# Taking the first level of the RWKV triangular inverse from the transposed pair matrix

## The chip, the cores and the metric

The kernel runs on one core of a Trainium2 chip. The number reported is the device time of one execution in microseconds (us), as a median of several. The names of the engines in the profile: PE is TensorE (PEld its weight loads), DVE is VectorE, ACT is ScalarE, POOL is GpSimd, SP is the engine that issues most DMAs.

## The reference, cut to what matters

The program is three transformer layers on one sequence of 512 tokens. Two layers are of one kind (mLSTM, gated linear attention, sparse attention); the third has an RWKV-7 branch beside a differential attention branch, then a feed-forward part. The change lies in the RWKV branch, whose core is a recurrence over tokens, run forwards and backwards for 8 heads of width 64:

```
def step(state, inp):
    r_t, w_t, k_t, v_t, kk_t, a_t = inp
    sa = jnp.einsum('bhij,bhj->bhi', state, -kk_t)
    state = (state * w_t[:, :, None, :]
             + sa[..., None] * (kk_t * a_t)[:, :, None, :]
             + v_t[..., None] * k_t[:, :, None, :])
    y_t = jnp.einsum('bhij,bhj->bhi', state, r_t)
    return state, y_t
...
y = (rwkv7_scan(r_h, decay[:, :, 0], k_dir[:, :, 0], v_h, kk, a[:, :, 0], False)
     + rwkv7_scan(r_h, decay[:, :, 1], k_dir[:, :, 1], v_h, kk, a[:, :, 1], True))
```

The kernel does not step through tokens. It cuts the sequence into 8 chunks of 64 tokens. Inside a chunk the feedback of one token on the next is a strictly triangular 64x64 matrix A of inner products (the decayed removal keys, here `kap`, against the decayed replacement keys, here `bet`), and the chunk needs the inverse of I + A.

## The kernel before, in words

**Stages.** The kernel is a chain of stages with a barrier between them. Most stages are large matrix products at full width. `rwkv_stage` is one stage of about 175 us, in which all matrices are small.

**Tiling of the stage.** It has four rounds (`PER = 4`, the loop variable `i`). One round treats two heads for all 8 chunks, in both directions; a direction is a "way", `w.d` 0 or 1, with four PSUM banks each. A tile named `AT`, `BT`, `M`, `MT`, `MbT`, `MkT` or `T1` is 128 partitions by 512 columns: 16 matrices of 64x64, eight side by side in the upper 64 partitions and eight in the lower.

**The head of a round, on PE.** `within` multiplies keys with keys, chunk by chunk. Called at line 1858 with `cols == 2` it makes 64x128 products: first `bet` against `kap` and `rho` together, which gives the transposed pair matrix `AT` (and `MbT`), later `kha` against the same, which gives `BT` and `MkT`. Called at line 1860 it makes the untransposed matrix A, 64x64, into banks 0 and 1. The order on PE is: AT for both ways, A for both ways, BT for both ways (the second after ACT has copied AT out of the banks they share).

**The head on the other engines.** ACT copies AT and BT out of PSUM (line 2111, one instruction of 1024 columns each, semaphores `at_copied`, `bt_copied`). DVE makes the start of the inverse from A: line 2282 multiplies it with the mask of level 0 (the pairs of neighbouring tokens), line 2284 subtracts the result from the identity; `m_ready` then lets PE go on. POOL masks BT in place (line 2193) and, at the start of each round but the first, finishes the state matrices of the round before (lines 2167 and 2168).

**The levels.** The inverse is doubled in five levels. In each, and for both ways: `by_level` (line 1869) multiplies AT and M, DVE masks the product into T1 (line 2289), PE transposes M (line 1885) and ACT copies it to MT (line 2136), `by_inverse` (line 1878) multiplies MT and T1, DVE subtracts from M (line 2295). The last level is done in transposed form (lines 1893 and 2299). Between these stand small products for the round before or after (`beside`).

**The tail.** After the levels come the products with the inverse (line 2038), then a long row of 64x64 products, lines 2051 to 2074, and right behind them the AT products of the next round. ACT copies the results of lines 2071 and 2074 at line 2151 (`gh_copied`), POOL then works on them (lines 2167, 2168).

The order on each engine is the order of the code; the engines meet only at semaphores. `then_inc` counts a semaphore up when the instruction is done, `wait_ge` holds the engine's queue.

Of the kernel before, what the change touches and what calls it, by code (L numbers as in the profile page):

```python
# [8 lines left out]
ALU = mybir.AluOpType  # L9
# [3 lines left out]
P = 128  # L13
# [5 lines left out]
CHUNK = 64  # L19
# [49 lines left out]
class Chain:  # L69


    def __init__(self, eng, sem):
        self.eng, self.sem, self.n = eng, sem, 0
# [20 lines left out]
def by_tile(x):  # L94
    return x.rearrange("p (t n) -> p t n", n=P)
# [1619 lines left out]
HALF = (slice(0, 64), slice(64, 128))  # L1715
# [7 lines left out]
def every(mask):  # L1723

    return mask.rearrange("p (a n) -> p a n", a=1).broadcast_to([P, NCH, CHUNK])
# [16 lines left out]
class Way:  # L1742
# [7 lines left out]
    def __init__(self, m, d):  # L1750
        self.d, self.bank = d, 4 * d
        mats = m.rw_mats[:, 8 * d:8 * d + 8, :]
        self.AT, self.BT, self.M, self.MT, self.MbT, self.MkT, _, self.T1 = (mats[:, n, :] for n in range(8))
        self.AT_MbT, self.BT_MkT = (mats[:, n:n + 5:4, :] for n in range(2))
        self.nPZ = mats[:, 0:2, :].rearrange("p a (t n) -> p (a t) n", n=P)
        self.keys = m.rw_keys[d]
        self.kap, self.bet, self.kha = (self.keys[:, n, :] for n in range(3))
        self.rho = [self.keys[:, 3 + n, :] for n in range(2)]
        self.kap_rho = [self.keys[:, 0:4 + n:3 + n, :] for n in range(2)]
        tok = m.rw_tok[d]  # L1760
        self.cat = tok[:, 0:2, :].rearrange("p a (t n) -> p (a t) n", n=P)
        self.bet_t, self.kha_t = by_tile(tok[:, 2, :]), by_tile(tok[:, 3, :])
        first = m.rw_first[d]
        self.kap_of, self.bet_of, self.kha_of = ((lambda i, n=n: first[n] if i == 0 else self.keys[:, n, :]) for n in range(3))
        self.rho_of = lambda i: first[3] if i == 0 else self.rho[i % 2]
        self.kap_rho_of = lambda i: m.rw_first_pair[d] if i == 0 else self.kap_rho[i % 2]
        self.sg, self.a, self.cum = m.rw_temps[d]
        self.ex_in, self.ex_neg = m.tmp[:, 2 * d, :], m.tmp[:, 2 * d + 1, :]
        self.ex = self.sg if d == 0 else m.rs[:, 2, :]
        self.g, self.h = m.rw_gh[d]  # L1770
        self.gh = m.arena[:, 34 + d:38 + d:2, :]
        self.strict, self.incl = (m.cstrict_f, m.cincl_f) if d == 0 else (m.cstrict_b, m.cincl_b)
        self.levT = (m.clevel_b, m.clevel_f)[d]

    def at(self, n):

# [21 lines left out]
def pair_place(c):  # L1798

    return 64 * (2 * (c % T) + c // T)  # L1800


def turn_of(t):

    return 2 * (t % 2) + t // 2
# [12 lines left out]
def rwkv_stage(nc, m, ahead):  # L1818
# [4 lines left out]
    ways = [Way(m, 0), Way(m, 1)]  # L1823
    ch = chunked
    PER = 4
    SCAN_AT, EX_AT = (4, 6), (12, 16)

    names = ("at_ready", "at_copied", "a_ready", "bt_ready", "bt_copied", "bt_masked", "mb_masked", "mk_masked", "bv_ready", "bv_copied",
             "m_ready", "mt_ready", "t1_ready", "t1_copied", "x_ready", "xt_ready", "pz_ready", "pz_copied",
             "ry_ready", "ry_taken", "gh_ready", "gh_copied", "gh_taken", "k_ready", "kha_ready", "rate_ready", "ex_ready", "exp_ready",  # L1830
             "tok_ready")
    with stage(nc, "dve_own", "pool_own", "lora_ready", "turn_ready", "sig_ready", "gs_ready", "s_ready", "yi_ready", "yi_taken",
# [12 lines left out]
        def _(pe):  # L1845
            def bank(w, n):
                return m.ps[:, w.bank + n, :]

            def within(w, banks, lhsT, rhs, cols):

                for t in range(T):
                    for p, hh in QUADS:
                        c = 2 * t + p
                        cs, at = slice(c * 64, c * 64 + 64), turn_of(t) * P
                        ps = slice(pair_place(c), pair_place(c) + 64)
                        if cols == 2:
                            out = m.ps[HALF[p], w.bank + banks[hh], at:at + P].rearrange("p (a n) -> p a n", a=2)
                            ins = pe.matmul(out, lhsT[HALF[hh], cs], rhs[HALF[hh], :, ps], start=True, stop=True)
                        else:
                            ins = pe.matmul(m.ps[HALF[p], w.bank + banks[hh], at:at + 64], lhsT[HALF[hh], ps], rhs[HALF[hh], cs],  # L1860
                                            start=True, stop=True)
                return ins

            def by_level(w):

                for j in range(T):
                    for p, h in QUADS:
                        cols = slice(64 * (2 * j + h), 64 * (2 * j + h) + 64)
                        ins = pe.matmul(m.ps[HALF[h], w.bank + p, 64 * j:64 * j + 64], w.AT[HALF[p], cols], w.M[HALF[p], cols],
                                        start=True, stop=True)  # L1870
                return ins
# [123 lines left out]
            for i in range(PER):  # L1995
                more = i + 1 < PER
                for w in ways:
                    if i:
                        pe.wait_ge(sem[f"k_ready{w.d}"], 3 * i)
                        pe.wait_ge(sem[f"ry_taken{w.d}"], 2 * i)  # L2000
                    within(w, (2, 3), w.bet_of(i), w.kap_rho_of(i), 2).then_inc(sem[f"at_ready{w.d}"], 1)
                for w in ways:
                    if i:
                        pe.wait_ge(sem[f"gh_copied{w.d}"], i)
                    within(w, (0, 1), w.kap_of(i), w.bet_of(i), 1).then_inc(sem[f"a_ready{w.d}"], 1)
                for w in ways:
                    pe.wait_ge(sem[f"at_copied{w.d}"], i + 1)
                    if i:
                        pe.wait_ge(sem[f"kha_ready{w.d}"], i)
                    within(w, (2, 3), w.kha_of(i), w.kap_rho_of(i), 2).then_inc(sem[f"bt_ready{w.d}"], 1)  # L2010
                for n in range(1, LAST + 1):
                    for w in ways:
                        pe.wait_ge(sem[f"m_ready{w.d}"], LAST * i + n)
                        by_level(w).then_inc(sem[f"t1_ready{w.d}"], 1)
                        if n == 1:
                            pe.wait_ge(sem[f"bt_copied{w.d}"], i + 1)
                        if w.d == 1 and n in (2, 3) and more:
                            pe.wait_ge(sem["sig_ready"], 4 * i + 2 * (n - 1))
                        if n == 4 + w.d:
                            pe.wait_ge(sem[f"bv_copied{w.d}"], i + 1)  # L2020
                        turned_inverse(w).then_inc(sem[f"xt_ready{w.d}"], 1)
                    beside(i, 2 * n - 2)
                    for w in ways:
                        pe.wait_ge(sem[f"t1_copied{w.d}"], LAST * i + n)
                        pe.wait_ge(sem[f"mt_ready{w.d}"], (LAST + 1) * i + n)
                        if n < LAST:
                            by_inverse(w).then_inc(sem[f"x_ready{w.d}"], 1)
                        else:
                            transposed(w).then_inc(sem[f"xt_ready{w.d}"], 1)
                    beside(i, 2 * n - 1)  # L2030
                for w in ways:
# [3 lines left out]
                    for j in range(T):  # L2035
                        for h, p in QUADS:
                            x = 2 * j + p
                            ins = pe.matmul(m.ps[HALF[p], w.bank + h, j * P:j * P + P],
                                            w.MT[HALF[h], 64 * x:64 * x + 64], w.cat[HALF[h], x, :], start=True, stop=True)
                    ins.then_inc(sem[f"pz_ready{w.d}"], 1)  # L2040
                for w in ways:
# [11 lines left out]
                    for t in range(T):  # L2053
# [4 lines left out]
                        for p, hh in QUADS:  # L2058
                            ins = pe.matmul(m.ps[HALF[hh], w.bank + 2 + p, 256 + t * 64:320 + t * 64],
                                            w.nPZ[HALF[p], at_slot(hh, t), 64:P],  # L2060
                                            w.MbT[HALF[p], 256 * hh + 64 * turn_of(t):256 * hh + 64 * turn_of(t) + 64], start=False, stop=True)
                    ins.then_inc(sem[f"ry_ready{w.d}"], 1)
                for w in ways:
# [5 lines left out]
                    for t in range(T):  # L2069
# [3 lines left out]
                        for p, hh in QUADS:  # L2073
                            ins = pe.matmul(m.ps[HALF[hh], w.bank + p, 256 + t * 64:320 + t * 64], w.bet_t[HALF[p], t, HALF[hh]],
                                            w.nPZ[HALF[p], at_slot(hh, t), 64:P], start=False, stop=True)
# [134 lines left out]
        def _(dve):  # L2210
            own = Chain(dve, sem["dve_own"])
            eye = every(m.eye64)
# [64 lines left out]
            dve.tensor_scalar(m.cols[:, 24:28], m.c2("k_a", 4), -1.0, 1.0, ALU.mult, ALU.add).then_inc(sem["rest_ready"], 1)  # L2277
            for i in range(PER):
                for w in ways:
                    a = m.ps[:, w.bank:w.bank + 2, :].rearrange("p a (t x n) -> p (a t) x n", x=2, n=64)  # L2280
                    dve.wait_ge(sem[f"a_ready{w.d}"], i + 1)
                    own.op(dve.tensor_tensor(ch(w.M), a[:, :, 0, :], every(w.levT[:, 0:64]), ALU.mult))
                    own.wait()
                    dve.tensor_tensor(ch(w.M), eye, ch(w.M), ALU.subtract).then_inc(sem[f"m_ready{w.d}"], 1)
                for n in range(1, LAST + 1):
                    for w in ways:
                        mask = w.levT[:, n * 64:n * 64 + 64].rearrange("q (a j n) -> q a j n", a=1, j=1).broadcast_to([P, 2, T, CHUNK])
# [871 lines left out]
```

## Time and profile before

| what | value |
|---|---|
| median of 3 runs | 2307.98 us (2306.52 to 2308.14) |
| the profiled execution's own time | 2306.07 us |
| its span, first to last instruction | 2304.3 us |
| outside the span | 1.8 us |
| PE busy | 2214.3 us, 96% |
| DVE, ACT, POOL busy | 1139.4, 967.9, 926.4 us |
| the stage of the change | from about 1358 to 1533 us of the span |

Times in the rows are microseconds from the start of the span, unless they are marked ns. In a timeline row the first number is the start, the second the time from the first start to the last end of the group, and `xN` the number of instructions in it. Each matmul of 32-bit numbers that the code writes stands twice in the trace: 16 matmuls of 64x64 are `x32`. A wait in brackets is idle time before the row, with what ended it; "issue" is idle time that the profile can lay on no other engine.

### The profile page before, as it was taken

The page shows a single profiled execution, that of the slowest core. Times are in us where ns is not written, and L with a number is a line of the kernel's source. Part 1 is how long each engine was busy: PE and PEld are TensorE (multiplying, and loading weights), DVE is VectorE, ACT ScalarE, POOL GpSimd, SP SyncE. Part 2 cuts the span into 40 slices and gives each one's busy share as a digit, 9 for nine tenths or more (in the row PEclk, how much of TensorE's full clock was granted, in tenths as well). Part 3 has the DMA queues.
Part 4 walks back from the last instruction along what each step waited for, and adds up shares of the span by engine and source line. Part 5 has one row for each costly group of instructions (what it writes and reads, how often), then busy time and mean ns, then how long its engine had stood idle before and what let it go on. Part 6 is the DMA issues. An engine that isn't in the chain of part 4 may idle for free. (4 is left out here: it accounts for less than half of the span.)

```text
span 2304.3 us, 36016 instructions
## 1 busy us (share of the span) xinstructions
PE 2214.3 (96%) x14926; PEld 1713.3 (74%) x14926; DVE 1139.4 (49%) x1925; ACT 967.9 (42%) x1384; POOL 926.4 (40%) x705
## 2 busy tenths in 40 slices
PE   7999999999999999999999988879999999999997
PEld 5776777787877857767878777767666788888885
DVE  5554843344246549342443686644544757216425
ACT  5433355445354233553452445534367242222243
POOL 4342243334543413433345445533332455445453
PEclk9999999999999999999999999999999999999998
DMA  4221222222322302222132300012121233323322
GB/s 155 86 92 37 68 88 74 64 74 80 97 83 79 95 19 85 89 65 73 65 106 92 101 20 4 4 31 84 64 65 55 92 97 97 100 92 101 100 92 73
DMA packets 50558, 175.03 MB, mean 76 GB/s; under 512 B 6036, under 2 KB 7004, under 8 KB 50396
## 3 DMA queue, kind: packets, MB, share of 16 engines
q1 hardware_dynamic: 50396, 172.73, 23.5%
q8 instruction: 118, 1.93, 0.3%
q14 instruction: 44, 0.36, 0.0%
HBM read 170.60 MB, written 2.11 MB: 75 GB/s over the span
## 5 line engine op out<-in xcount | busy, mean ns | idle before, releaser
L349 POOL TENSOR_TENSOR w_low<-work,w_high 128x512 fp32r<-128x512 f32 x622 | 834.9, 1363 | 1243.1 <-ACT w_high L298 1243.1
L279 PE MATMUL ps<-x_high_tiles,w_high 128*128 128x512 f32 x1544 | 624.5, 404 | 18.0 <-POOL w_low L349 11.5
L298 ACT ACTIVATE w_high<-work 128x1024 fp32r<-128x1024 f32 x311 | 329.3, 1059 | 734.2 <-PE ps L279 730.4
L279 PE MATMUL ps<-x_low_tiles,w_high 128*128 128x512 f32 x1544 | 603.7, 391 | 0.8 <-DVE x_low_tiles L371 0.8
L279 PE MATMUL ps<-x_high_tiles,w_low 128*128 128x512 f32 x1544 | 603.4, 391 | 0.0
L279 PE MATMUL ps<-arena_parts,w_high 128*128 128x512 f32 x1264 | 397.6, 391 | 4.3 <-DVE arena L437 1.6
L279 PEld LDWEIGHTS ps<-x_high_tiles,w_high 128*128 128x128 f32 x1544 | 290.8, 188 | 119.2 <-issue 44.6
L279 PEld LDWEIGHTS ps<-x_low_tiles,w_high 128*128 128x128 f32 x1544 | 290.7, 188 | 64.2 <-DVE x_low_tiles L371 1.6
L279 PEld LDWEIGHTS ps<-x_high_tiles,w_low 128*128 128x128 f32 x1544 | 291.2, 189 | 63.1 <-issue 6.0
L279 PEld LDWEIGHTS ps<-arena_parts,w_high 128*128 128x128 f32 x1264 | 237.3, 188 | 56.8 <-issue 3.2
L279 PE MATMUL ps<-arena_parts,w_low 128*128 128x512 f32 x608 | 236.6, 389 | 0.0
L441 DVE TENSOR_TENSOR xT_sb<-ps,xT_sb 128x512 f32<-128x512 f32 x40 | 27.6, 691 | 249.3 <-PE ps L279 249.3
L279 PEld LDWEIGHTS ps<-arena_parts,w_low 128*128 128x128 f32 x608 | 114.2, 188 | 24.1 <-issue 0.7
L279 PE MATMUL ps<-w_high,x_high_tiles 128*128 128x512 f32 x288 | 118.2, 410 | 2.6 <-POOL w_low L349 2.6
L279 PE MATMUL ps<-w_high,x_low_tiles 128*128 128x512 f32 x288 | 112.4, 390 | 0.0
L279 PE MATMUL ps<-w_low,x_high_tiles 128*128 128x512 f32 x288 | 112.3, 390 | 0.0
L437 DVE TENSOR_TENSOR arena<-ps,arena 128x512 f32<-128x512 f32 x32 | 22.1, 691 | 123.2 <-ACT ps L436 123.2
L835 DVE SCALAR_TENSOR_TENSOR arena<-ps,small,arena 128x511 f32<-128x511 f32 (+2 forms) x96 | 71.9, 749 | 3.4
L279 PEld LDWEIGHTS ps<-w_high,x_high_tiles 128*128 128x128 f32 x288 | 54.0, 188 | 25.6 <-issue 11.0
L422 ACT ACTIVATE arena<-ps 128x512 f32<-128x512 f32 x84 | 47.9, 596 | 59.1 <-PE ps L279 59.0
L831 DVE TENSOR_SCALAR arena<-ps,small 128x512 f32<-128x512 f32 x32 | 25.8, 807 | 76.2 <-PE ps L279 76.2
L279 PEld LDWEIGHTS ps<-w_low,x_high_tiles 128*128 128x128 f32 x288 | 54.1, 188 | 12.5 <-issue 2.2
(446 smaller groups left out, 2790.5 us busy)
## 6 DMA issues: line engine op xcount, KB each, us to landing
work<-w_first SPq DMA_DIRECT2D x178, 512.0 KB, 3.6
work<-w_second SPq DMA_DIRECT2D x134, 512.0 KB, 3.6
xT_sb<-xT SPq DMA_DIRECT2D x8, 256.0 KB, 6.6
outT<-arena SPq DMA_DIRECT2D x8, 256.0 KB, 2.1
arena<-distance_bias SPq DMA_DIRECT2D x4, 256.0 KB
small<-small SPq DMA_DIRECT2D x1, 815.5 KB, 5.1
arena<-consts SPq DMA_DIRECT2D x1, 544.0 KB, 3.7
base<-consts SPq DMA_DIRECT2D x1, 512.0 KB
```

The source lines that it names most:

```text
L279: ins = pe.matmul(out, lhsT, rhs, start=(n == 0 and k == 0 and q == 0), stop=(n == unit["granules"] - 1 and k == len(ops[i]) - 1 and q == 2))
L298: act.activation(m.wh[:, split_of(g), :], m.raw[:, raw_of(g), :], ACT.Copy).then_inc(sem["high_ready"], 1)
L349: pool.tensor_tensor(m.wl[:, split_of(g), part], m.raw[:, raw_of(g), part], m.wh[:, split_of(g), part].bitcast(F32), ALU.subtract).then_in ...
L422: return dict(act=lambda e, ps: e.activation(dst, ps, ACT.Copy))
L437: dve=lambda e, ps, own: e.tensor_tensor(dst, ps, dst, ALU.mult))
L441: return dict(dve=lambda e, ps, own: e.tensor_tensor(dst, ps, dst, ALU.add))
L831: own.op(dve.tensor_scalar(acc, ps, cw[:, 48 + i:49 + i], cb[:, i:i + 1], ALU.mult, ALU.add))
L835: ins = dve.scalar_tensor_tensor(out=acc[:, back:S], in0=ps[:, 0:S - back], scalar=c, in1=acc[:, back:S], op0=ALU.mult, op1=ALU.add)
```

## The change

The untransposed products and their semaphore `a_ready` go. DVE takes the transposed matrix `AT` that ACT has copied, masks it with the level-0 mask of the other orientation (`lev0`), subtracts it from the identity into T1, and transposes T1 into M by its 32x32 block transpose. All that is not zero there lies in 2x2 blocks on the diagonal, so that transposing every 32x32 block in place is the transpose of each 64x64 matrix. The work on the two ways is interleaved: both masks, both subtractions, both transposes. PE's wait for `gh_copied` (ACT has emptied banks 0 and 1 of the round before) moves from the products of A to the first level.

```diff
-        self.levT = (m.clevel_b, m.clevel_f)[d]
+        self.levT, self.lev0 = (m.clevel_b, m.clevel_f)[d], (m.clevel_f, m.clevel_b)[d][:, 0:CHUNK]
...
                 for w in ways:
                     if i:
                         pe.wait_ge(sem[f"k_ready{w.d}"], 3 * i)
                         pe.wait_ge(sem[f"ry_taken{w.d}"], 2 * i)
-                    within(w, (2, 3), w.bet_of(i), w.kap_rho_of(i), 2).then_inc(sem[f"at_ready{w.d}"], 1)
-                for w in ways:
-                    if i:
-                        pe.wait_ge(sem[f"gh_copied{w.d}"], i)
-                    within(w, (0, 1), w.kap_of(i), w.bet_of(i), 1).then_inc(sem[f"a_ready{w.d}"], 1)
+                    within(w, w.bet_of(i), w.kap_rho_of(i)).then_inc(sem[f"at_ready{w.d}"], 1)
                 for w in ways:
                     pe.wait_ge(sem[f"at_copied{w.d}"], i + 1)
...
-                    within(w, (2, 3), w.kha_of(i), w.kap_rho_of(i), 2).then_inc(sem[f"bt_ready{w.d}"], 1)
+                    within(w, w.kha_of(i), w.kap_rho_of(i)).then_inc(sem[f"bt_ready{w.d}"], 1)
                 for n in range(1, LAST + 1):
                     for w in ways:
                         pe.wait_ge(sem[f"m_ready{w.d}"], LAST * i + n)
+                        if n == 1 and i:
+                            pe.wait_ge(sem[f"gh_copied{w.d}"], i)
                         by_level(w).then_inc(sem[f"t1_ready{w.d}"], 1)
...
             for i in range(PER):
                 for w in ways:
-                    a = m.ps[:, w.bank:w.bank + 2, :].rearrange("p a (t x n) -> p (a t) x n", x=2, n=64)
-                    dve.wait_ge(sem[f"a_ready{w.d}"], i + 1)
-                    own.op(dve.tensor_tensor(ch(w.M), a[:, :, 0, :], every(w.levT[:, 0:64]), ALU.mult))
-                    own.wait()
-                    dve.tensor_tensor(ch(w.M), eye, ch(w.M), ALU.subtract).then_inc(sem[f"m_ready{w.d}"], 1)
+                    dve.wait_ge(sem[f"at_copied{w.d}"], i + 1)
+                    dve.tensor_tensor(ch(w.T1), ch(w.AT), every(w.lev0), ALU.mult).then_inc(sem[f"pairs_ready{w.d}"], 1)
+                for w in ways:
+                    dve.wait_ge(sem[f"pairs_ready{w.d}"], 2 * i + 1)
+                    dve.tensor_tensor(ch(w.T1), eye, ch(w.T1), ALU.subtract).then_inc(sem[f"pairs_ready{w.d}"], 1)
+                for w in ways:
+                    dve.wait_ge(sem[f"pairs_ready{w.d}"], 2 * i + 2)
+                    dve.transpose(w.M, w.T1).then_inc(sem[f"m_ready{w.d}"], 1)
```

On PE, at the head of the second round, this stood (`ps` is PSUM, `work` holds the keys and matrices; here a matmul of the code counts once):

```order
L2074 MATMUL ps<-work,arena 64x64 x4
L1858 MATMUL ps<-work 64x128 x32
L1860 MATMUL ps<-work 64x64 x32
L1858 MATMUL ps<-work 64x128 x32
L1869 MATMUL ps<-work 64x64 x16
L1885 MATMUL ps<-base,work 128x128 x4
```

and this stands now, with line 1857 for 1858, 1865 for 1869, 1881 for 1885 and 2068 for 2074:

```order
L2068 MATMUL ps<-work,arena 64x64 x4
L1857 MATMUL ps<-work 64x128 x64
L1865 MATMUL ps<-work 64x64 x16
L1881 MATMUL ps<-base,work 128x128 x4
```

The 32 products of A are gone, and the BT products stand right behind the AT products. On DVE, at the same place, stood:

```order
L2282 TENSOR_TENSOR work<-ps,arena 128x512
L2284 TENSOR_TENSOR work<-arena,work 128x512
L2282 TENSOR_TENSOR work<-ps,arena 128x512
L2284 TENSOR_TENSOR work<-arena,work 128x512
L2289 TENSOR_TENSOR work<-ps,arena 128x2x4x64 x2
```

and now stands:

```order
L2275 TENSOR_TENSOR work<-work,arena 128x512 x2
L2278 TENSOR_TENSOR work<-arena,work 128x512 x2
L2281 STREAM_TRANSPOSE work<-work 128x512 x2
L2286 TENSOR_TENSOR work<-ps,arena 128x2x4x64 x2
```

Four instructions became six, the two ways are interleaved, and the first of each pair reads SBUF instead of PSUM.

## Rows read from the trace of the kernel before

**Rows 1.** The page: span, and PE's busy time.
```profile
span 2304.3 us, 36016 instructions
PE 2214.3 (96%) x14926; PEld 1713.3 (74%) x14926; DVE 1139.4 (49%) x1925; ACT 967.9 (42%) x1384; POOL 926.4 (40%) x705
```
**Rows 2.** Windows: stretch, length, busy time and instructions by engine, granted clock, DMA.
```profile
1404.00:1452.00 48.00, 41.76 (x1572) 36.17 (x1567) 31.68 (x53) 27.21 (x41) 27.80 (x21) 1.00 0.02 4
```
**Rows 3.** Waits of PE in the stage: total, times, longest.
```profile
PE ps L1858 <- issue: 4.1, 5, 1.1
...
PE ps L1869 <- DVE work L2295: 2.1, 5, 0.7
```
**Rows 4.** Timeline of the first round's head.
```profile
1362.83 1.96 PE L1860 MATMUL ps<-arena 64*64 64x64 f32 x64
1363.14 1.02 ACT L2111 ACTIVATE work<-ps 128x1024 f32<-128x1024 f32 x1 [0.68 <-PE ps L1858]
1363.99 0.69 DVE L2282 TENSOR_TENSOR work<-ps,arena 128x512 f32<-128x512 f32 x1 [4.43 <-PE ps L1860]
1364.72 0.69 DVE L2284 TENSOR_TENSOR work<-arena,work 128x512 f32<-128x512 f32 x1
1365.33 0.68 DVE L2282 TENSOR_TENSOR work<-ps,arena 128x512 f32<-128x512 f32 x1
...
1366.47 0.65 PE L1869 MATMUL ps<-work 64*64 64x64 f32 x32
```
**Rows 5.** Timeline of the second round's head: PE, ACT, POOL.
```profile
1406.81 1.94 ACT L2111 ACTIVATE work<-ps 128x1024 f32<-128x1024 f32 x2 [1.30 <-PE ps L1858]
...
1411.09 0.22 PE L1869 MATMUL ps<-work 64*64 64x64 f32 x1
...
1406.42 1.28 POOL L2167 TENSOR_TENSOR arena<-arena 128x512 f32<-128x512 f32 x1
1407.64 1.06 POOL L2168 TENSOR_TENSOR arena<-arena 128x512 f32<-128x512 f32 x1
```
**Rows 6.** The same of the third and the fourth round: ACT's second copy, PE's first level.
```profile
1454.65 1.02 ACT L2111 ACTIVATE work<-ps 128x1024 f32<-128x1024 f32 x1 [1.06 <-PE ps L1858]
1457.87 0.67 PE L1869 MATMUL ps<-work 64*64 64x64 f32 x32
...
1502.37 1.02 ACT L2111 ACTIVATE work<-ps 128x1024 f32<-128x1024 f32 x1 [0.20 <-PE ps L1858]
1505.59 0.31 PE L1869 MATMUL ps<-work 64*64 64x64 f32 x3
```
**Rows 7.** Timeline of two breaks in PE's work, and windows from break to break.
```profile
1406.35 1.22 PE L1858 MATMUL ps<-work 64*64 64x128 f32 x34 [1.12 <-issue]
...
1410.07 1.25 PE L1858 MATMUL ps<-work 64*64 64x128 f32 x35 [0.70 <-issue]
...
1399.20:1402.70 3.50, 2.09 (x128) 1.96 (x128) 1.74 (x3) 0.60 (x1) 0.00 (x0) 1.00 0.02 5
1402.70:1406.30 3.60, 2.50 (x127) 2.36 (x128) 0.00 (x0) 2.05 (x2) 2.11 (x2) 1.00 0.02 5
1406.30:1410.00 3.70, 3.02 (x127) 2.78 (x127) 1.81 (x3) 1.94 (x2) 2.41 (x3) 1.00 0.02 4
```
**Rows 8.** DMA of the window 1396 to 1412 us: queue, packets, MB, share.
```profile
q8 instruction: 5, 0.08, 2.0%
```
**Rows 9.** Timeline of POOL and DVE at the end of the first round; groups of DVE instructions by form.
```profile
1394.97 1.78 POOL L2185 TENSOR_TENSOR work<-arena,tmp 128x512 f32<-128x512 f32 x1 [2.70 <-ACT work L2090]
...
1395.53 1.76 DVE L2239 TENSOR_TENSOR work<-arena,tmp 128x512 f32<-128x512 f32 x1
...
L2239 DVE TENSOR_TENSOR work<-work,tmp 128x512 f32<-128x512 f32 x3 | 2.1, 684 | 0.0
...
L731 DVE TENSOR_SCALAR arena<-xT_sb,small 128x512 f32<-128x512 f32 x32 | 14.1, 484 | 0.6
```
**Rows 10.** Timeline: PE waits for DVE in the second round. Windows: the clock in the fourth.
```profile
1426.71 1.26 DVE L2295 TENSOR_TENSOR work<-work,ps 128x512 f32<-128x512 f32 x2
1427.43 0.39 PE L1869 MATMUL ps<-work 64*64 64x64 f32 x10 [0.66 <-DVE work L2295]
...
1498.00:1501.40 3.40, 3.40 (x98) 3.26 (x91) 0.00 (x0) 1.28 (x2) 1.55 (x2) 0.50 0.02 5
```

More of the change, by code:

```diff
@@ L1826, in rwkv_stage @@
     SCAN_AT, EX_AT = (4, 6), (12, 16)
-    names = ("at_ready", "at_copied", "a_ready", "bt_ready", "bt_copied", "bt_masked", "mb_masked", "mk_masked", "bv_ready", "bv_copied",
-             "m_ready", "mt_ready", "t1_ready", "t1_copied", "x_ready", "xt_ready", "pz_ready", "pz_copied",
+    names = ("at_ready", "at_copied", "bt_ready", "bt_copied", "bt_masked", "mb_masked", "mk_masked", "bv_ready", "bv_copied",
+             "pairs_ready", "m_ready", "mt_ready", "t1_ready", "t1_copied", "x_ready", "xt_ready", "pz_ready", "pz_copied",
              "ry_ready", "ry_taken", "gh_ready", "gh_copied", "gh_taken", "k_ready", "kha_ready", "rate_ready", "ex_ready", "exp_ready",
@@ L1847, in bank, with within @@
                 return m.ps[:, w.bank + n, :]
-            def within(w, banks, lhsT, rhs, cols):
+            def within(w, lhsT, rhs):
                 for t in range(T):
@@ L1855, in within @@
                         ps = slice(pair_place(c), pair_place(c) + 64)
[L1856 to L1861, printed above, removed]
+                        out = m.ps[HALF[p], w.bank + 2 + hh, at:at + P].rearrange("p (a n) -> p a n", a=2)
+                        ins = pe.matmul(out, lhsT[HALF[hh], cs], rhs[HALF[hh], :, ps], start=True, stop=True)
                 return ins
```

## The prediction

> **What bounds the kernel now.** I read the page first: PE is busy for 2214.3 of 2304.3 us, 96% [rows 1], so that PE's time is the kernel's time almost everywhere, and what happens outside the RWKV stage is untouched by the diff. Then the windows of that stage: in one round of 48.0 us PE is busy for 41.8, DVE for 31.7, ACT for 27.2 and POOL for 27.8 [rows 2]. PE leads there too, but it works in short pieces that hang on the others. The list of waits shows how little: in four rounds PE waits 2.1 us in front of the first product of a level (line 1869) for DVE, and 4.1 us in the key products for "issue", so for no engine [rows 3]. The change touches only the head of each round, four times, so I went through the four heads in the timeline, with one question: what does the first product of level 1 (line 1869) wait for? In none of the four is a wait shown before it. It starts when PE is through with AT, A and BT; DVE has M ready before that. In the first round DVE's second instruction for way 0 ends at 1364.72 + 0.69 = 1365.41, and line 1869 starts at 1366.47 [rows 4]. The removed products are thus on PE's path, and the reader should expect a gain; the question is what takes their place.
>
> **What goes.** 32 products of the code, 64 in the trace, in each round. The first round's 64 fill 1.96 us, at a lower clock than later [rows 4]; in the second round the stretch from 1406.3 to 1410.0 has 127 matmuls in 3.02 us of busy time [rows 7], so 64 of them are worth at most 1.5 us of PE. If PE alone decided, the four heads would be shorter by about 1.96 + 3 x 1.1 (3 x 1.5 as upper end) = 5 to 6.5 us.
>
> **What comes in their place.** M now hangs on a new chain: AT's second copy on ACT, then on DVE mask 1, subtraction 0, subtraction 1, transpose 0, and only then line 1869 of way 0. DVE's instructions of 128x512 with no dependence start 0.61 us apart (line 2284 at 1364.72, line 2282 at 1365.33) and last 0.69 [rows 4]. From the end of AT's copy for way 1: 0.07 us to start, 3 x 0.61 us until the first transpose starts, its duration d, and 0.07 us to PE. The 0.07 is from a wait that is in the trace: two DVE instructions take 1.26 us from 1426.71, the second needs about 0.61, the first thus ends near 1427.36, and PE starts at 1427.43 [rows 10]; I take the same from ACT to DVE. No transpose of DVE is in the trace. Its nearest rows: 0.48 us for a 128x512 instruction with one SBUF source (line 731), 0.68 with two (line 2239), 1.76 us for the same when POOL works beside it [rows 9]. It moves 512 columns of 32-bit numbers and reads one tile; I take the middle one, d = 0.69, and keep 0.48 and 1.76 as ends. The Trainium skill, in "VectorE: DVE Perf Modes", section "The three transpose paths", gives 311 ns for 128x128 in 16-bit numbers on VectorE; with the 384 further columns at one a cycle of 0.96 GHz, which is an estimate from that page, 512 columns would take 0.71 us. No run here shows it yet.
>
> The chain is then 0.07 + 1.83 + 0.69 + 0.07 = 2.66 us. In the trace of before, line 1869 started after the end of that same copy:
> - first round: 1366.47 - 1364.16 = 2.31 [rows 4]
> - second: 1411.09 - (1406.81 + 1.94) = 2.34 [rows 5]
> - third and fourth: 1457.87 - 1455.67 = 2.20, and 1505.59 - 1503.39 = 2.20 [rows 6]
>
> So line 1869 comes 0.35, 0.32, 0.46 and 0.46 us later against the copy: +1.6 us in all. What was PE's work becomes PE's idling, a little longer than the work was. For way 1 nothing more is late: its transpose ends 0.61 us behind way 0's, and PE comes to it about 1.2 us after way 0, behind the four transposes of line 1885. BT's copies come earlier than before by about a microsecond and are not late. ACT's and POOL's order is unchanged. The wait for `gh_copied` now stands before the first level; what it waits for ends before AT's copy on the same engine, and costs nothing. With d = 0.48 the sum is +0.8, with d = 1.76 it is +1.6 + 4 x 1.07 = +5.9, and way 1 suffers too (below).
>
> **PE's breaks.** The copy itself may come earlier. PE stops at 1402.7, 1406.3 and 1410.0 for no engine, each time after 127 or 128 matmuls with as many weight loads, and 3.5 to 3.7 us apart [rows 7]; in the same 16 us the queue marked "instruction" moves five packets, 0.08 MB [rows 8]. I read these breaks as PE waiting for its own instructions: about one packet of 16 KB per break. Work between breaks is 2.1 to 3.0 us, the rest is waiting. 64 matmuls fewer in every round move each later break by half such a block. Before the second and the fourth round the breaks fall at another place, before the third and behind the stage at the same place as now. The most that this can bring is one break less before AT is done, 1.1 us [rows 7]; then ACT's copies of the round before hold AT's copies up. I take -0.5 us each for the second and the fourth round, bounds 0 and -1.1.
>
> **POOL's neighbourhood.** Line 2282 read PSUM, the new mask reads two SBUF tiles, while POOL is at lines 2167 and 2168 until 1408.70 in the second round [rows 5]. DVE's line 2239, two SBUF sources, takes 0.68 us alone and 1.76 with POOL working from 1394.97 on [rows 9]: 1.08 us more. The first mask has slack behind it, since the second waits for AT's second copy; the second meets POOL at most in one or two rounds. I take +0.3 us in all, bounds 0 and 4.3 (1.08 in each round). The skill's page "SBUF — State Buffer", section "Who interferes with whom", says that VectorE with two SBUF inputs and GpSimd exclude each other for whole instructions; by it the transpose, which has one source, would be free of POOL unless it runs in a two-port mode, and the sum would stay as it is. These rows agree for the two-source instruction and say nothing of the transpose.
>
> **The sum.** +1.6 - 1.0 + 0.3 = +0.9 us on the profiled execution: span 2304.3 becomes 2305.2, its own time 2306.07 becomes 2307.0. The median of before is 1.9 us above that execution's time, so that the predicted median is 2307.98 + 0.9 = 2308.9 us. A difference under 0.2%, 4.6 us, is what I count as none.
>
> **Rivals.**
> 1. PE decides after all: the removed products come off the end. That needs M ready when BT is done. For it: today line 1869 waits for nobody. Against: the chain above is longer than AT-to-level in all four rounds. If the transpose takes 0.48 us, both rounds with shifted breaks gain their full 1.1 us, and the half-speed stretch at 1498.0 to 1501.4, where 98 matmuls take 3.40 us [rows 10], does not come again (about -1.5 us), the sum is +0.8 - 2.2 - 1.5 = -2.9 us, 2305.1. Only if PE's instructions were the bound everywhere in the stage, so that two full blocks of 3.5 us fall away, would it be -7 us, 2301; the levels, where PE waits for nobody's instructions, speak against it. 2301: chance 6%.
> 2. The transpose is slow, from its own nature or because POOL is at line 2193 beside it (which starts as soon as BT is copied, now earlier). This ends slower. The place is line 1869 of both ways at the head of each round. With d = 1.76, way 0 is 1.07 us later than in my sum and way 1's M comes at 1.83 + 2 x 1.76 behind the mask, 0.5 us later than PE gets there: 1.6 us a round, 6.4 in all, 2315. It decides from d = 1.6 on: there the total passes 4.6 us. Chance 10%.
> 3. The clock. PE now idles about 1.5 us before line 1869 instead of working. The clock stood at 0.50 for 3.4 us in the fourth round [rows 10], behind several gaps of 1 to 2 us. If the new gap brings one such stretch in each of three rounds, and each costs some 1.2 us, the sum is +4.5, 2312.5. Chance 8%, mostly still within the bound.
>
> **How the numbers follow.** My forecast, a difference of a microsecond or two either way, has 76%, the rivals 6, 10 and 8. Range 2305.0 to 2313.0: the lower end is the sum with the short transpose and both breaks, the upper one lets in the third rival and half of the way to the second. Faster by over 0.2%: 6%. Slower by over 0.2%: 11%, rival 2 and a little of 3. Within: 83%.
>
> **What would show it.** In the profile of after: line 1865 (the old 1869) waits for DVE's transpose in all four rounds, with 1 to 2 us each, 4 to 7 in all, where before no wait stood. The transpose takes 0.65 to 0.75 us. From the end of AT's second copy to line 1865 it is 2.6 to 2.7 us. PE's busy time falls by some 4 us and the span does not. The breaks marked "issue" in the second and fourth round stand before or behind the key products and not in them. I am wrong if line 1865 starts right behind the BT products, if the transpose takes over 1 us, or if the time between line 1869 of one round and the next (46.8 us now from the second to the third, 47.7 to the fourth [rows 5, 6]) moves by over 1 us.

## The result, and the profile after

The changed kernel takes 2315.47 us (median of 6, 2312.01 to 2318.59) against 2308.06 (2306.52 to 2309.38): ratio 1.0033, 95% interval 1.0020 to 1.0046. It is 7.4 us slower, where I had forecast +0.9 and a range up to 2313. The profiled execution, the one looked at below, took 2318.41 us, 2.9 above that median; the one of the kernel before took 2306.07, 2.0 below its own. The profiles thus lie 12.3 us apart and the medians 7.4, and what is split up below is the 12.3.

The page of the kernel after, answering to [rows 1]:

```profile
span 2316.6 us, 35518 instructions
PE 2218.8 (96%) x14670; PEld 1715.4 (74%) x14670; DVE 1151.8 (50%) x1933; ACT 968.0 (42%) x1384; POOL 930.4 (40%) x705
```

256 matmuls are gone, yet PE's busy time has grown by 4.5 us and DVE's by 12.4: eight more instructions of about 0.7 us explain 5.5 of those, the rest is instructions that have become longer. The waits of PE in the stage (in total, times, longest), answering to [rows 3]:

```profile
PE ps L1865 <- DVE work L2281: 12.3, 4, 4.4
...
PE ps L1865 <- DVE work L2292: 2.1, 5, 0.7
...
PE ps L1857 <- issue: 1.0, 1, 1.0
```

The new wait at the first level is where I put it, four times, but with 12.3 us instead of 4 to 7. The breaks for "issue" in the key products have gone from 4.1 us to 1.0. Which instruction makes the new wait long? The forms of DVE's new instructions in the stage (count, busy us, mean ns):

```profile
L2278 DVE TENSOR_TENSOR work<-arena,work 128x512 f32<-128x512 f32 x8 | 10.5, 1356 | 0.0
L2275 DVE TENSOR_TENSOR work<-work,arena 128x512 f32<-128x512 f32 x8 | 7.8, 986 | 22.5 <-ACT work L2105 22.5
L2281 DVE STREAM_TRANSPOSE work<-work 128x512 f32<-128x512 f32 x8 | 5.2, 682 | 0.0
```

The transpose is innocent: 682 ns, as I had priced it (0.69). The subtraction, an instruction that the kernel had before and that took 0.69 us [rows 4], has a mean of 1356, and the new mask one of 986. The timeline of the second round's head, first ACT's copies of AT, then DVE, POOL and PE's first level (start, length, engine, line):

```profile
1406.36 1.93 ACT L2105 ACTIVATE work<-ps 128x1024 f32<-128x1024 f32 x2
...
1407.41 2.40 DVE L2275 TENSOR_TENSOR work<-work,arena 128x512 f32<-128x512 f32 x2 [6.61 <-ACT work L2105]
1409.73 3.45 DVE L2278 TENSOR_TENSOR work<-arena,work 128x512 f32<-128x512 f32 x2
1413.10 1.29 DVE L2281 STREAM_TRANSPOSE work<-work 128x512 f32<-128x512 f32 x2
...
1407.77 1.49 POOL L2162 TENSOR_TENSOR arena<-arena 128x512 f32<-128x512 f32 x1
1409.70 2.93 POOL L2187 TENSOR_TENSOR work<-work,arena 128x512 f32<-128x512 f32 x2 [0.44 <-ACT work L2105]
...
1413.85 1.13 PE L1865 MATMUL ps<-work 64*64 64x64 f32 x32 [4.40 <-DVE work L2281]
```

POOL begins to mask BT at 1409.70 and DVE to subtract at 1409.73; the two subtractions last 3.45 us together instead of 1.28, and POOL's two instructions 2.93 instead of 2.51. Ahead of them the two masks take 2.40 us instead of about 1.3, beside POOL's line 2162. In the kernel before the subtraction and POOL's mask did not meet:

```profile
1408.88 0.69 DVE L2284 TENSOR_TENSOR work<-arena,work 128x512 f32<-128x512 f32 x1
...
1410.20 0.69 DVE L2284 TENSOR_TENSOR work<-arena,work 128x512 f32<-128x512 f32 x1
...
1411.64 2.51 POOL L2193 TENSOR_TENSOR work<-work,arena 128x512 f32<-128x512 f32 x2 [2.94 <-ACT work L2111]
```

There DVE was through at 1410.89, since M came from A ahead of BT, and POOL had BT only at 1411.64, since the products of A stood in front of BT. The change has moved both, DVE's subtraction later and POOL's mask earlier, onto each other.

The chain can be measured in each round, from the end of AT's second copy to the first level: 2.60, 5.56, 3.67 and 5.56 us, where the kernel before had 2.31, 2.34, 2.20 and 2.20. That is 8.3 us more. The copies themselves end 2.7 us earlier after the start of the key products, summed over the rounds (3.16 instead of 4.57 us in the second, 3.17 instead of 4.41 in the fourth), where a break of PE has left the key products. Together this is the +5.7 of the heads in the table below.

The clock is the second part. Windows of the levels, from line 1865 (1869) to the products with the inverse, rounds two, three and four, of the kernel after (stretch, length, busy time by engine, granted clock last but two):

```profile
1413.80:1444.80 31.00, 30.00 (x880) 24.85 (x880) 21.46 (x39) 16.38 (x26) 14.33 (x11) 0.91 0.02 4
1464.20:1495.60 31.40, 30.43 (x884) 25.25 (x884) 21.49 (x39) 16.38 (x26) 15.54 (x12) 0.90 0.01 4
1516.10:1544.80 28.70, 28.11 (x872) 24.37 (x872) 16.80 (x34) 9.83 (x17) 4.14 (x4) 0.90 0.02 4
```

and of the kernel before:

```profile
1411.10:1439.80 28.70, 27.76 (x889) 23.03 (x881) 20.88 (x38) 17.62 (x28) 17.57 (x13) 1.00 0.02 5
1457.90:1486.50 28.60, 27.66 (x888) 22.92 (x879) 20.88 (x38) 17.28 (x27) 17.41 (x13) 1.00 0.02 5
1505.60:1533.80 28.20, 26.52 (x885) 23.00 (x875) 16.27 (x33) 10.74 (x18) 7.30 (x6) 1.00 0.02 5
```

The same work takes 2.3 and 2.8 us more in the second and third round, at a mean clock of 0.91 and 0.90 instead of 1.00: behind PE's wait of 4.4 us the first 32 matmuls of the level take 1.13 us instead of 0.65 [rows 4]. In the second round the granted clock is still 1.00 at 1412.0 us, in the middle of the wait, 0.50 from 1412.5 to 1419.0, and 1.00 again from 1419.5.

I cut every trace at three places of each round, by the start of PE's first instruction there: the key products, the first level, the products with the inverse; the last part runs to the next stage. Sums over four rounds, in us:

| kernel | heads | levels | tails | to the end | median | ratio to before, interval |
|---|---|---|---|---|---|---|
| before | 27.1 | 111.8 | 57.9 | 748.1 | 2308.1 | |
| after | 32.8 | 117.1 | 59.2 | 748.6 | 2315.5 | 1.0033, 1.0020 to 1.0046 |
| no_products | 19.7 | 111.9 | 59.6 | 748.2 | 2300.5 | 0.9971, 0.9960 to 0.9982 |
| pool_later | 27.2 | 111.6 | 61.2 | 748.5 | 2308.2 | 1.0005, 0.9996 to 1.0015 |
| fill | 33.4 | 110.9 | 59.4 | 748.6 | 2312.4 | 1.0020, 1.0011 to 1.0030 |
| way_by_way | 22.3 | 120.6 | 59.7 | 748.2 | 2312.1 | 1.0021, 1.0011 to 1.0031 |
| psum_pairs | 27.9 | 111.5 | 60.0 | 748.4 | 2308.1 | 0.9996, 0.9987 to 1.0005 |
| psum_both | 26.3 | 110.8 | 61.2 | 748.4 | 2306.4 | 0.9991, 0.9982 to 1.0000 |
| way_later | 22.4 | 114.0 | 60.4 | 748.6 | 2305.9 | 0.9988, 0.9978 to 0.9997 |
| way_psum | 21.2 | 113.7 | 60.3 | 748.6 | 2304.8 | 0.9988, 0.9979 to 0.9998 |
| way_psum_later | 21.1 | 112.2 | 59.1 | 748.4 | 2303.0 | 0.9982, 0.9973 to 0.9991 |

Before to after, on the profiled executions: heads +5.7, levels +5.3, tails +1.3, behind the stage +0.5, less 0.4 by which the stage began earlier: 12.4, the difference of the spans (12.3). The times of the stretches come from one profiled execution each. The mean granted clock is on record for every execution: 0.987 to 0.991 in the six of the changed kernel, 0.987 in the profiled one, and 0.991 to 0.993 in 27 of the kernel before. The changed kernel is thus the slower clocked, but its profile lies at the low end, and how much of the median's 7.4 us is clock is not known.

### The profile page after: what moved, and what is told of

Read it like the earlier page. It is cut to its first block and busy times, and to the rows that moved or that the text cites. A ratio compares the mean times of both kernels' runs of the same rounds, so it can differ in the third digit from the quotient of the medians.

```text
span 2316.6 us, 35518 instructions
## 1 busy us (share of the span) xinstructions
PE 2218.8 (96%) x14670; PEld 1715.4 (74%) x14670; DVE 1151.8 (50%) x1933; ACT 968.0 (42%) x1384; POOL 930.4 (40%) x705
## 5 line engine op out<-in xcount | busy, mean ns | idle before, releaser
L422 ACT ACTIVATE arena<-ps 128x512 f32<-128x512 f32 x84 | 47.9, 597 | 59.1 <-PE ps L279 59.0
```

The costliest lines, as they stand in the source:

```text
L422: return dict(act=lambda e, ps: e.activation(dst, ps, ACT.Copy))
```

## The experiments

All but `no_products` start from the changed kernel. The intervals above compare each with runs of the kernel before on the same chip, whose medians were 2307.1 for the first four experiments, 2308.0 for the next four and 2306.9 for the last.

**pool_later: POOL out of the way.**

```diff
+                for w in ways:
+                    pool.wait_ge(sem[f"m_ready{w.d}"], LAST * i + 1)
                 for w in ways:
                     pool.wait_ge(sem[f"bt_copied{w.d}"], i + 1)
```

> The changed kernel, but POOL starts masking BT only when DVE's transposes of both ways are done. Theory (POOL and DVE's two-source instructions exclude each other, and the idle time this makes on PE then halves its clock): the four-by-two subtractions of DVE go from 1.75 us to 0.69 us, in rounds two to four the head gets shorter by about 2 us each, and the time falls from 2315.5 to between 2309 and 2312; the 6.8 us stretches at half clock behind the heads go or get fewer. Rival A (the slow clock has nothing to do with the wait, it comes from the changed rhythm of PE): subtractions shorter, but the three slow stretches stay, 2311 to 2313. Rival B (subtractions are slow by their operands and not by POOL): nothing changes, 2315.

2308.16 us: the ratio to the kernel before falls from 1.0033 to 1.0005, some 6.5 us, with one wait on another engine. The subtractions take 682 ns on the mean, and PE's wait halves; the second way's mask still meets POOL in the second and fourth round (1.48 us):

```profile
L2280 DVE TENSOR_TENSOR work<-arena,work 128x512 f32<-128x512 f32 x8 | 5.1, 682 | 0.0
...
PE ps L1865 <- DVE work L2283: 6.5, 4, 1.9
```

Of the three slow stretches behind the heads one is left, in the second round and half as long (its levels take 30.2 us, those of the third 28.7). Rival B is out: same instruction, same operands, half the time. Rival A is out for two of the three stretches. The time came out below the range I gave, since the heads fell by 5.6 us and the levels by 5.5; the tails took back 2.0.

**fill: the removed work put back, unread.**

```diff
+                for w in ways:
+                    if i:
+                        pe.wait_ge(sem[f"gh_copied{w.d}"], i)
+                    for t in range(T):
+                        for p, hh in QUADS:
+                            c = 2 * t + p
+                            pe.matmul(m.ps[HALF[p], w.bank + hh, turn_of(t) * P:turn_of(t) * P + 64],
+                                      w.kap_of(i)[HALF[hh], pair_place(c):pair_place(c) + 64],
+                                      w.bet_of(i)[HALF[hh], c * 64:c * 64 + 64], start=True, stop=True)
                 for n in range(1, LAST + 1):
```

> The changed kernel, with the products of A made again behind the BT products, into banks that nobody reads, so that PE has 1.1 us of work (64 matmuls of the trace) in the gap before the first level. Theory (PE's removed work is worth nothing, its idle gap costs clock): no slower than the changed kernel although it does all that was removed; 2310 to 2315.5. Rival (the removed work still pays, the gap is harmless): slower than the changed kernel by about 4 us, 2319.

2312.42 us: with 256 matmuls more than the changed kernel, 3 us less by the medians, though the intervals of the two ratios overlap (1.0020 to 1.0046, and 1.0011 to 1.0030). The theory, no slower than the changed kernel, holds; that it is faster is not settled by the times. In the profiles the heads are not shorter (33.4 against 32.8), the levels are, by 6.2 us, and the mean clock of its ten executions is 0.991 to 0.993; its windows of the second and third round:

```profile
1414.40:1443.10 28.70, 27.72 (x880) 22.98 (x880) 21.47 (x39) 16.25 (x26) 15.55 (x12) 1.00 0.02 4
1463.10:1491.80 28.70, 27.72 (x880) 22.98 (x880) 21.47 (x39) 16.25 (x26) 15.54 (x12) 1.00 0.02 4
```

880 matmuls in 28.70 us at 1.00, where the changed kernel has 880 in 31.00 at 0.91. The longest single wait of PE for the transpose is 1.6 us here and was 4.4. That makes the clock, not the levels' work, the cause of the 5.3 us there: the same stretch costs 2.3 to 2.7 us more at the lower clock. It is not a pure test of the clock: only the second way's subtraction meets POOL in this kernel (mean 1222 ns), so the wait is shorter for that reason too.

**no_products: the ceiling.** From the kernel before, without the products of A and, with them, without the level-0 part of the inverse, so that its result is not the inverse. PE's wait for `gh_copied` moves to the first level, as in the change; the diff here leaves that out.

```diff
-                for w in ways:
-                    if i:
-                        pe.wait_ge(sem[f"gh_copied{w.d}"], i)
-                    within(w, (0, 1), w.kap_of(i), w.bet_of(i), 1).then_inc(sem[f"a_ready{w.d}"], 1)
...
-                    dve.wait_ge(sem[f"a_ready{w.d}"], i + 1)
-                    own.op(dve.tensor_tensor(ch(w.M), a[:, :, 0, :], every(w.levT[:, 0:64]), ALU.mult))
+                    dve.wait_ge(sem[f"at_ready{w.d}"], i + 1)
+                    if i:
+                        dve.wait_ge(sem[f"gh_copied{w.d}"], i)
+                    own.op(dve.scalar_tensor_tensor(out=ch(w.M), in0=a[:, :, 0, :], scalar=0.0,
+                                                    in1=every(w.levT[:, 0:64]), op0=ALU.mult, op1=ALU.mult))
```

> The kernel before without the products of A and without a wait for them: DVE's line 2282 multiplies what stands in the banks with zero, so that the start of the inverse is the identity (left out: the level-0 part). It bounds what the removal could have brought. Theory: PE's 64 matmuls are on the path of every head, the level follows BT directly; 1.1 to 1.9 us a round, 2308.0 becomes 2302 to 2304. Rival (PE's instruction supply sets the pace of the stage): 1.75 us a round and more, 2299 to 2301. Rival (removing PE work brings nothing since ACT's copies take its place): 2306 to 2308.

2300.54 us, 0.29% below the kernel before. The heads fall by 7.4 us, of which the tails give back 1.7. The products were on PE's path in every head, as I had read; the value, 6.6 us against the same chip's 2307.1, is the upper end that I had worked out for PE alone (6.5). The time is below the range I gave and inside that of the rival, PE's instruction supply. The levels did not move, so that supply does not set their pace; but in the heads, which held breaks of 1.12 and 0.70 us [rows 7], the products and the breaks went together, and this run does not tell them fully apart: 5.0 of the 7.4 us lie behind the end of AT's second copy, 2.4 ahead of it, where the products never stood. A change of this kind could thus have brought 6.6 us.

**way_by_way: DVE's order.**

```diff
                 for w in ways:
                     dve.wait_ge(sem[f"at_copied{w.d}"], i + 1)
                     dve.tensor_tensor(ch(w.T1), ch(w.AT), every(w.lev0), ALU.mult).then_inc(sem[f"pairs_ready{w.d}"], 1)
-                for w in ways:
                     dve.wait_ge(sem[f"pairs_ready{w.d}"], 2 * i + 1)
                     dve.tensor_tensor(ch(w.T1), eye, ch(w.T1), ALU.subtract).then_inc(sem[f"pairs_ready{w.d}"], 1)
-                for w in ways:
                     dve.wait_ge(sem[f"pairs_ready{w.d}"], 2 * i + 2)
                     dve.transpose(w.M, w.T1).then_inc(sem[f"m_ready{w.d}"], 1)
```

> The changed kernel with DVE's six instructions in the order mask, subtract, transpose of way 0, then of way 1. Way 0 no longer waits for AT's second copy. Theory: the first level of way 0 starts right behind BT, some 3 us earlier in rounds two to four; way 1 then waits, with its subtraction beside POOL (1.75 us), about 1.5 us; 2315.5 becomes 2309 to 2312. Rival (way 1 decides, since both must be through before the second half of the level): 2313 to 2315.

2312.05 us, just above my range's end. The heads fall to 22.3 us, but the levels grow to 120.6: what way 0 gains, way 1 loses inside the first level, and in two rounds a stretch at half clock is in it (0.79 on the mean in 1411 to 1418 us, 0.76 in 1512 to 1519). DVE and POOL in its second round:

```profile
1409.96 1.55 DVE L2275 TENSOR_TENSOR work<-work,arena 128x512 f32<-128x512 f32 x1
1411.55 1.64 DVE L2277 TENSOR_TENSOR work<-arena,work 128x512 f32<-128x512 f32 x1
1413.22 0.71 DVE L2279 STREAM_TRANSPOSE work<-work 128x512 f32<-128x512 f32 x1
...
1409.70 2.94 POOL L2187 TENSOR_TENSOR work<-work,arena 128x512 f32<-128x512 f32 x2 [0.95 <-ACT work L2105]
```

Way 1's mask and subtraction both meet POOL, its transpose again does not suffer, although POOL is at work until 1418 us there.

**psum_pairs and psum_both: one operand in PSUM.** POOL is left as it is.

```diff
-   dve.tensor_tensor(ch(w.T1), ch(w.AT), every(w.lev0), ALU.mult)
+   if i:
+       dve.wait_ge(sem[f"gh_copied{w.d}"], i)
+   dve.tensor_tensor(ch(m.ps[:, w.bank, :]), ch(w.AT), every(w.lev0), ALU.mult)
-   dve.tensor_tensor(ch(w.T1), eye, ch(w.T1), ALU.subtract)
+   dve.tensor_tensor(ch(w.T1), eye, ch(m.ps[:, w.bank, :]), ALU.subtract)
```

In `psum_both` the mask also reads AT from its banks, `at[:, :, 0, :]`, and PE's BT products wait for `pairs_ready` at `2 * i + 1` instead of `at_copied`.

> The changed kernel, but DVE writes the masked pairs to the way's first PSUM bank (free by then) and subtracts from there, so that the subtraction has one operand in SBUF and one in PSUM. POOL is as in the changed kernel and masks BT beside it. Theory (only DVE instructions with two operands in SBUF and POOL hold each other up): the subtractions take 0.69 us although POOL works, the masks stay slow (0.95 to 1.5 us), the gap before the first level is about 2 us a round shorter, 2309 to 2311. Rival (POOL's activity slows whatever DVE does then, or an instruction that writes SBUF): subtractions stay at 1.75 us, 2315.

> As the one before, and the mask reads AT from PSUM too, after ACT's copy of it; PE's BT products wait for that mask instead of the copy. No DVE instruction of the new chain has two SBUF operands. Theory: mask 0.69, subtraction 0.69, transpose 0.68 in every round, POOL back at 1.27 us, and BT 0.7 us later, which the chain hides: 2308 to 2310, as I forecast for the change itself. Rival (BT's delay is not hidden): 2311 to 2313.

2308.05 and 2306.37 us. In `psum_pairs` the masks stay slow and the subtractions are quick:

```profile
L2277 DVE TENSOR_TENSOR ps<-work,arena 128x512 f32<-128x512 f32 x8 | 7.9, 994 | 24.1 <-ACT work L2105 24.1
...
L2280 DVE TENSOR_TENSOR work<-arena,ps 128x512 f32<-128x512 f32 x8 | 5.1, 677 | 0.0
```

In `psum_both` both are quick (699 and 679 ns). Its second round, DVE and POOL:

```profile
1409.22 0.70 DVE L2278 TENSOR_TENSOR ps<-ps,arena 128x512 f32<-128x512 f32 x1 [0.22 <-ACT work L2105]
1409.83 1.27 DVE L2281 TENSOR_TENSOR work<-arena,ps 128x512 f32<-128x512 f32 x2
1411.02 1.30 DVE L2284 STREAM_TRANSPOSE work<-work 128x512 f32<-128x512 f32 x2
...
1408.66 1.04 POOL L2162 TENSOR_TENSOR arena<-arena 128x512 f32<-128x512 f32 x1
1411.33 2.51 POOL L2187 TENSOR_TENSOR work<-work,arena 128x512 f32<-128x512 f32 x2 [1.62 <-ACT work L2105]
```

The second mask and the first subtraction overlap POOL's line 2162 and nobody is longer for it; the transposes run beside line 2187 in 1.30 us, and POOL takes 2.51 for two as in the kernel before. From the second mask to the first transpose it is 1.80 us (I had 1.83). This kernel is the change as I had pictured it. From the end of AT's second copy to the first level it takes 2.59 us in all four rounds, where `psum_pairs` has 3.39 in the second and fourth: so much, 1.6 us in all, the slow mask alone cost. Its heads are 0.8 us shorter than before, and its time is below the range that I gave for this run, as is that of `psum_pairs`: BT's later start is hidden.

**way_later, way_psum, way_psum_later: the means together.** The edits are those above: the order way by way with POOL's later mask, the same with the subtraction from PSUM, and all three.

> DVE's order way by way and POOL's BT mask behind both transposes, together. Each brought a part alone (2312.1 and 2308.2 against 2315.5). Theory: they remove the same gap by two means, way by way also frees way 0 of the wait for the second copy, so that the sum is below either: 2304 to 2307, faster than the kernel before. Rival (way 1's chain of three instructions decides in both): 2308.

> DVE's order way by way, with the subtraction from PSUM, POOL unchanged. Theory: way 1's mask still meets POOL at BT (1.7 us), its subtraction does not (0.69 instead of 1.64): 1 us less of waiting a round than way by way alone, 2308 to 2310. Rival (the gap before way 1 is set by something else): 2312.

> All three means together: DVE's order way by way, the subtraction from PSUM, POOL's BT mask behind both transposes. What is left of the collisions in way_psum is way 1's mask beside POOL. Theory: that mask falls from above 1.4 us to 0.69 us, way 1 of the first level comes up to 0.7 us a round earlier, 2304.8 becomes 2302.5 to 2304, near the 2300.5 of the kernel that leaves out the products and the level-0 part. Rival (way 1 of the first level is set by way 0's products and transposes on PE by now, and POOL's later mask costs elsewhere): 2304.5 to 2306.

2305.94, 2304.83 and 2303.04 us. The last beats the kernel before by 0.18% (interval 0.09 to 0.27%) and the changed kernel by some 12 us. It and `way_later` came out inside their ranges, `way_psum` 3 us below its own, for a reason that its trace shows: way 1's mask, expected at 1.7 us beside POOL, took 0.67 in three of the four rounds (1.78 in the fourth): way 0's subtraction is quick now, and way 1's mask begins before POOL has BT (1409.26 against 1409.72 in the second round). So there was little left for POOL's later mask to gain, and the ratios of `way_psum` and `way_psum_later`, 0.9988 and 0.9982, do not differ clear of noise. In the last kernel the second round reads:

```profile
1406.48 0.95 DVE L2279 TENSOR_TENSOR ps<-work,arena 128x512 f32<-128x512 f32 x1 [6.61 <-ACT work L2105]
...
1408.83 0.67 DVE L2279 TENSOR_TENSOR ps<-work,arena 128x512 f32<-128x512 f32 x1
...
1410.25 0.71 DVE L2283 STREAM_TRANSPOSE work<-work 128x512 f32<-128x512 f32 x1
...
1411.10 2.50 POOL L2189 TENSOR_TENSOR work<-work,arena 128x512 f32<-128x512 f32 x2 [2.76 <-DVE work L2283]
```

Six DVE instructions in 4.5 us, of which one (0.95) still meets POOL, at the state matrices of the round before.

## Why the prediction was wrong, by its steps

**The removed products.** Right in the main: on PE's path, 5 to 6.5 us by rows; `no_products` gives 6.6, though part of it are the breaks.

**The new chain.** Right in its parts. The transpose takes 0.68 us; `psum_both` shows the chain at 2.59 us, 2.66 forecast, so that the term of +1.6 us measures +1.4. From the end of AT's second copy to the first level I had 2.66 us; in the changed kernel the copies of the second round end at 1408.29 (1406.36 + 1.93) and the level starts at 1413.85: 5.56.

**POOL's neighbourhood: the step that failed.** The prediction says of this: "The first mask has slack behind it, since the second waits for AT's second copy; the second meets POOL at most in one or two rounds. I take +0.3 us in all, bounds 0 and 4.3 (1.08 in each round)." I had the rule, from the Trainium skill and in a row (0.68 alone, 1.76 beside POOL [rows 9]), and applied it to one of the two instructions that it holds for. I looked for POOL's work where it stood in the old trace, lines 2167 and 2168, and for DVE instructions with a new operand. The subtraction had its old operands, and POOL's BT mask stood behind it in the old trace; the change moves both. In rounds two to four five of six subtractions take 1.74 to 1.78 us: in each of the second and fourth round this costs 2.16 us against `pool_later`, in the third 1.06, 5.4 us in all, for which the prediction had nothing. The mask itself was priced too low as well: way 1's meets POOL in two rounds, as the prediction allowed, and takes 1.48 us instead of 0.69 in each, 1.6 us for which it had taken 0.3. With the chain's own +1.4 these make the 8.3 us between copy and level, of which the earlier copies give back 2.7. `pool_later` takes the subtractions' part away from POOL's side, `psum_pairs` from DVE's; the heads return to 27.2 and 27.9, and to 26.3 in `psum_both`, where the mask is free too. The third round was spared one, since its first subtraction had begun before POOL did. "SBUF — State Buffer", section "Who interferes with whom", in the Trainium skill, says just this, that a VectorE instruction with two SBUF inputs and a GpSimd instruction that reads SBUF exclude each other; the kernels here agree for the two-source instructions (0.69 against 0.9 to 1.8 us), for those with one operand in PSUM, and for the transpose, which none of them shows slowed.

**Rival 1** did not come about: PE's first level waits in all four rounds. **Rival 2** had the right place on the time line, POOL's line 2193 starting earlier, and the wrong victim, the transpose. Its 6.4 us with 10% was nearest to what came.

**The clock, rival 3.** I took PE's gap as 1.5 us and gave three slow stretches 1.2 us each. The gap became up to 4.4 us, slow stretches came in all of rounds two to four (31.0 us at a mean of 0.91 and the 8.7 us of head before it at 0.92 make about 7 us at 0.5, the 1.2 GHz level), and the levels cost 5.3 us more in sum. Against `fill`, with the same work, a stretch costs 2.1 to 2.7 us instead of 1.2. It was no rival but a consequence: the collision makes the gap, and the slow clock comes with the gap: `pool_later`, whose longest wait is 1.9 us, has one half-speed stretch left behind the heads, and `fill`, whose longest is 1.6, has none in the levels.

**PE's breaks.** The breaks moved as forecast: in the second and fourth round none stands in the key products, and AT's copies end 1.4 and 1.2 us earlier after the start of the head. Over all rounds this is -2.7 us, where I had -1.0 and at most -1.1 in a round. Against it stand tails that are 1.3 us longer, and 1 to 3 us longer in every variant, `no_products` too. Whether the breaks only went over into the tails is open; breaks marked "issue" stand there in each (in the changed kernel 2.7 and 2.5 us at lines 2061 and 2065). That the instruction supply is their reason was not tested.

**The range and chances.** The upper end, 2313, took in rival 3 and half of rival 2, but not that they come together. Both come from one cause, so the chances of 10 and 8% should not have been priced as separate cases.

**The signs that I had named.** The transpose is quick and line 1865 waits, as I had said. But PE's busy time rose by 4.5 us instead of falling by 4, copy to level is 2.6 us in one round only, and the sign of being wrong came: from the first level of the second round to that of the third it is 50.4 us instead of 46.8, to the fourth 51.9 instead of 47.7.

**What stays open.** The clock's part is shown by `fill` with a shorter wait beside it, not alone, and in the profiled executions, not in the medians; and why every variant's tails are longer was not tried.

## What to carry to other kernels

When an edit moves work, put both engines' instructions on the new time line before pricing them: an instruction whose text has not changed may meet a neighbour it never met. Do so for every instruction that the hazard holds for, not only for the new ones. On VectorE ask of each instruction in a chain whether it has two SBUF operands and what GpSimd does at that time; a spare PSUM bank as intermediate, or one wait on GpSimd, is a cheap way out (some 7 us here). And a wait of some microseconds on TensorE can cost twice, once as a wait and once as the clock behind it: here 4.4 us of waiting, and 2.3 us more for the levels behind.

## What the runs showed that I had not expected

- Two subtractions of 0.69 us beside POOL instructions of 1.27 take 3.45 us instead of 1.28: they cost DVE 2.2 us, and POOL 0.4 in its first two instructions and 0.4 in the third (line 2189, 1.71 us from 1412.59), which the second subtraction still overlaps.
- The 32x32 block transpose of 128x512 in 32-bit numbers takes 0.66 to 0.71 us on VectorE, beside POOL or not.
- With unread products on PE in the gap the kernel was no slower, by the medians 3 us faster.
